# Adding the experts' biases in PSUM on VectorE instead of by small matmuls on TensorE, in a decoder layer with a mixture of experts

## What is computed

```python
def expert_block(args):
    xb, e = args
    gu = xb @ w_gu[e] + b_gu[e]
    x_glu = jnp.minimum(gu[:, 0::2], SWIGLU_LIMIT)
    x_lin = jnp.clip(gu[:, 1::2], -SWIGLU_LIMIT, SWIGLU_LIMIT)
    act = x_glu * jax.nn.sigmoid(SWIGLU_ALPHA * x_glu) * (x_lin + 1.0)
    return act @ w_dn[e] + b_dn[e]
```

## Time and profile before

| | |
|---|---|
| median of three runs | 2505.62 us (2504.82 to 2506.62) |
| the profiled execution, its own time | 2506.4 us |
| its span, first to last instruction | 2504.6 us |
| mean granted TensorE clock | 0.957 |
| TensorE busy | 2316.6 us, 92% |
| VectorE busy | 911.4 us, 36% |
| ScalarE busy | 349.1 us, 14% |
| GpSimd busy | 850.3 us, 34% |
| bytes moved by DMA | 521 MB, 208 GB/s over the span |
| first and last start of a matmul of the experts' first layer | 861.4 and 2466.6 us |

### The profile page before, as it was taken

The page is one execution under the profiler, slowest core; times in us unless marked ns, Lnnn a source line. Parts: engine busy times, 40 slices in busy tenths (PEclk is TensorE's granted clock), DMA queues, the critical chain, the costliest instruction groups (busy, mean ns, idle before and its releaser), DMA issues. The chain is left out here.

```text
span 2504.6 us, 84029 instructions
## 1 busy us (share of the span) xinstructions
PE 2316.6 (92%) x34310; PEld 1402.4 (56%) x34310; DVE 911.4 (36%) x3040; ACT 349.1 (14%) x927; POOL 850.3 (34%) x1649
## 2 busy tenths in 40 slices
PE   5899997999899299999999998999999999999994
PEld 3677885555544145464545565555555555555552
DVE  2212215776457423232323332333333333333333
ACT  0000004776511011000000000000000000000001
POOL 1000002554314523333333433334344343443433
PEclk8999997999999589999989999999999999999997
DMA  9421024000132472919393939395797799799994
GB/s 316 187 105 37 1 71 112 2 1 2 51 107 93 163 289 71 377 25 358 90 334 114 372 95 396 93 373 183 288 395 285 284 351 394 283 350 397 370 349 155
DMA packets 176316, 521.08 MB, mean 208 GB/s; under 512 B 26712, under 2 KB 56048, under 8 KB 176016
## 3 DMA queue, kind: packets, MB, share of 16 engines
q1 hardware_dynamic: 141504, 476.59, 49.7%
q0 software_dynamic: 33680, 40.20, 7.9%
q10 hardware_dynamic: 976, 2.23, 0.4%
HBM read 485.12 MB, written 32.30 MB: 207 GB/s over the span
## 5 line engine op out<-in xcount | busy, mean ns | idle before, releaser
L1540 PE MATMUL psum<-w_ring,xT 128*32 128x256 f32 x18304 | 1042.5, 382 | 7.4 <-DMA w_ring<-in_w_gate_up 7.4
L1540 PEld LDWEIGHTS psum<-w_ring,xT 128*32 128x32 f32 x18304 | 577.3, 111 | 402.4 <-DMA w_ring<-in_w_gate_up 14.4
L1552 PE MATMUL psum<-w_ring,actT 128*32 128x256 f32 x9152 | 537.4, 386 | 24.3 <-DMA w_ring<-in_w_down 24.0
L1552 PEld LDWEIGHTS psum<-w_ring,actT 128*32 128x32 f32 x9152 | 279.5, 111 | 243.2 <-DVE actT L1607 37.3
L1474 POOL TENSOR_TENSOR scalars<-scalars 128x1 f32<-128x1 f32 x578 | 110.4, 191 | 824.9 <-DVE xT L1611 624.9
L1598 DVE TENSOR_SCALAR glu<-psum 128x128 f32<-128x128 f32 x286 | 83.5, 292 | 618.1 <-PE psum L1540 607.2
L1590 ACT ACTIVATE sig<-glu 128x128 f32<-128x128 f32 x286 | 88.9, 311 | 1516.5 <-DVE glu L1598 1373.5
L1493 POOL DMA_INDIRECT x_rows<-y_out,scalars_i x145 | 233.9, 1613 | 40.6 <-issue 40.4
L1620 DVE SCALAR_TENSOR_TENSOR y_out<-psum,scalars,gate_q 128x256 f32<-128x256 f32 x143 | 69.2, 484 | 444.8 <-DMA x_rows<-y_out,scalars_i 224.1
L675 POOL TENSOR_SCALAR scores<-scores,coef 128x64 f32<-128x64 f32 (+5 forms) x128 | 132.8, 1053 | 160.6 <-DVE coef L887 160.6
L1483 POOL DMA_INDIRECT x_gathered<-h_rows,scalars_i x144 | 152.9, 1062 | 83.1 <-issue 83.1
(11 more groups left out here) (228 smaller groups left out, 1985.0 us busy)
## 6 DMA issues: line engine op xcount, KB each, us to landing
w_ring<-in_w_gate_up SPq DMA_DIRECT2D x256, 1024.0 KB
w_ring<-in_w_down SPq DMA_DIRECT2D x128, 1024.0 KB
ada<-in_w_ada SPq DMA_DIRECT2D x24, 1024.0 KB, 8.0
xt<-in_x SPq DMA_DIRECT2D x8, 512.0 KB, 7.0
w_uv_then_w_out<-in_w_in SPq DMA_DIRECT2D x4, 1024.0 KB, 12.8
x_rows_in<-in_x SPq DMA_DIRECT2D x8, 512.0 KB, 4.7
x_rows<-x SPq DMA_DIRECT2D x8, 512.0 KB, 2.9
h_rows<-h SPq DMA_DIRECT2D x8, 512.0 KB
```

Of the source, the lines that this page charges most:

```text
L1540: last = nc.tensor.matmul(psU[h][j * BLK:(j + 1) * BLK, :], xT[:, k, :], w[:, j], start=False, stop=(k == KD - 1))
L1552: last = nc.tensor.matmul(psO[m * BLK:(m + 1) * BLK, :], actT[h][:, k, :], w[:, m * Q:(m + 1) * Q], start=False, stop=(h == 1 and k == KD ...
```

## The change

The first half's bias and the second layer's are no longer made by matmuls. VectorE adds them to the PSUM tiles: `b_up` to `psU[0]` before `glu`, and `b_dn` to `psO` before `y_out`. Only the second half's bias stays on TensorE, so `bias` shrinks to [96, 1024], and `split_bias` works on a third of the columns. For VectorE each bias must stand in all 32 partitions of a strip. `load_bias` does that on ScalarE's queue: eight DMAs per expert, each repeating one row (or a part of it) over 32 partitions. There are two buffers of each. The first two experts' loads are issued before the loop; from the second expert on, each expert's program begins with the loads for the next one, behind a wait for the last `y_out` of the expert before, which was the last reader of that buffer. VectorE waits for an expert's loads before its blocks. Some semaphores of `route` are merged, to the same effect.

```diff
@@ route: SyncE's loads
         for i in range(3):
-            sp.dma_start(b_rows[i * E:(i + 1) * E, 0:2 * D], b_gate_up).then_inc(s_b, 16)
-            sp.dma_start(b_rows[i * E:(i + 1) * E, 2 * D:3 * D], b_down).then_inc(s_b, 16)
+            sp.dma_start(b_rows[i * E:(i + 1) * E, :], b_gate_up[:, D:2 * D]).then_inc(s_b, 16)
...
@@ experts
+    b_up, b_dn = two("up_bias", [P, Q]), two("down_bias", [P, Q])
...
@@ experts: tensor
         def up(e, h):
-            w_bias = bias[:, h * D:(h + 1) * D].rearrange("p (b j c) -> p j b c", b=4, j=4)
-            for j in range(4):
-                nc.tensor.matmul(psU[h][j * BLK:(j + 1) * BLK, :], select[:, e:e + 1].to_broadcast([3 * E, BLK]), w_bias[:, j], start=True, stop=False)
+            w_bias = bias[:].rearrange("p (b j c) -> p j b c", b=4, j=4)
+            if h:
+                for j in range(4):
+                    nc.tensor.matmul(psU[h][j * BLK:(j + 1) * BLK, :], select[:, e:e + 1].to_broadcast([3 * E, BLK]), w_bias[:, j], start=True, stop=False)
...
                 pe.wait_ge(s_y, n + AHEAD)
-                for m in range(4):
-                    at = 2 * D + m * Q
-                    nc.tensor.matmul(psO[m * BLK:(m + 1) * BLK, :], select[:, e:e + 1].to_broadcast([3 * E, BLK]), bias[:, at:at + Q], start=True,
-                                     stop=False)
                 for h in range(2):
                     pe.wait_ge(s_actT[h], n + 1)
                     down(e, h)
...
@@ experts: scalar
+        def load_bias(p, done=None):
+
+            at = bias_place(p)
+            which = act.value_load(order[0:1, p:p + 1], min_val=0, max_val=E - 1)
+            if done is not None:
+                act.wait_ge(s_y, done)
+            up = b_gate_up[bass.ds(which, 1), 0:D].rearrange("a (b j c) -> (a j) b c", b=4, j=4)
+            down = b_down[bass.ds(which, 1), :].rearrange("a (m c) -> (a m) c", m=4)
+            for q in range(4):
+                rows = slice(q * BLK, (q + 1) * BLK)
+                act.dma_start(b_up[at][rows, :].rearrange("p (b c) -> p b c", b=4),
+                              up[q].partition_broadcast(BLK)).then_inc(s_bias[at], 16)
+                act.dma_start(b_dn[at][rows, :], down[q].partition_broadcast(BLK)).then_inc(s_bias[at], 16)
...
+        load_bias(0)
+        load_bias(1)
         for e in range(E):
             b = first_of(act, e)
             many = many_of(act, e)
+            if 1 <= e < E - 1:
+                load_bias(e + 1, b + AHEAD)
             with act.Fori(0, many) as i:
...
@@ experts: vector
             dve.wait_ge(s_up[h], b + 1)
+            if h == 0:
+                nc.vector.tensor_tensor(psU[0], psU[0], b_up[at][:], ALU.add).then_inc(s_added, 1)
+                dve.wait_ge(s_added, 3 * b + 1)
             nc.vector.tensor_scalar(glu[:], even, LIMIT, None, ALU.min).then_inc(s_glu[h], 1)
...
             dve.wait_ge(s_dn, b + 1)
+            nc.vector.tensor_tensor(psO, psO, b_dn[at][:], ALU.add).then_inc(s_added, 1)
+            dve.wait_ge(s_added, 3 * b + 3)
             dve.wait_ge(s_ysc, 16 * b + 16 * AHEAD + 16)
             nc.vector.scalar_tensor_tensor(y_out[:], psO, w_cur[:], gate2[:], ALU.mult, ALU.mult).then_inc(s_y, 1)
...
             dve.wait_ge(s_ids, 2 * e + 2)
+            at = bias_place(e)
+            dve.wait_ge(s_bias[at], 128 * (e // 2 + 1))
             with dve.Fori(0, many) as i:
```

More of the change, by code:

```diff
@@ L96, in layer_kernel @@
         counts = keep("block_counts", [P, 3, E], i32)
-        bias = keep("bias_parts", [3 * E, 3 * D], bf16)
+        bias = keep("lin_bias_parts", [3 * E, D], bf16)
         select = keep("select", [3 * E, E], bf16)
@@ L129, in layer_kernel @@
         with ExitStack() as s4:
-            s_w = experts(nc, s4, sem, psum, w_gate_up, w_down, k_quarter, list_d, h2_d, x1_d, mod_d, counts, bias, select, order)
+            s_w = experts(nc, s4, sem, psum, w_gate_up, w_down, b_gate_up, b_down, k_quarter, list_d, h2_d, x1_d, mod_d, counts, bias, select, order)
         with ExitStack() as s5:
@@ L1154, in body @@
                 pe.wait_ge(s_mask, TILES - 3)
-                nc.tensor.matmul(psR[:, 0:E], ones[:], total_b[1][:], start=True, stop=True).then_inc(s_part, 1)
+                nc.tensor.matmul(psR[:, 0:E], ones[:], total_b[1][:], start=True, stop=True).then_inc(s_cnt, 1)
             project(t, 0)
@@ L1299, in _ @@
         dve.wait_ge(s_first, 5)
[L1300 to L1301 removed]
+        nc.vector.scalar_tensor_tensor(scale2[:], scale2[:], 1.0, g2[:], ALU.add, ALU.mult).then_inc(s_first, 1)
+        dve.wait_ge(s_first, 6)
         def place_experts():
             first, second = place_f[:, 0, :], place_f[:, 1, :]
[L1305 removed]
+            dve.wait_ge(s_cnt, 1)
             ch.link(nc.vector.scalar_tensor_tensor(key[:], psR[:, 0:E], float(E), iota_e,
@@ L1353, in _, with experts @@
         ch.link(nc.vector.tensor_copy(counts[:], blocks_f[:]))
-def experts(nc, ctx, sem, psum, w_gate_up, w_down, k_quarter, list_d, h2_d, x1_d, mod_d, counts, bias, select, order):
+def experts(nc, ctx, sem, psum, w_gate_up, w_down, b_gate_up, b_down, k_quarter, list_d, h2_d, x1_d, mod_d, counts, bias, select, order):
     sb = lambda name, shape, dt=f32: ctx.enter_context(nc.sbuf_tensor(name, shape, dt))
@@ L1391, in experts @@
     s_spent = [sem(f"w_spent{c}") for c in range(CHUNKS)]
+    s_bias = [sem(f"bias_rows_loaded{i}") for i in range(2)]
     s_rows, s_quarter, s_ids = sem("slot_rows_loaded"), sem("quarter_added"), sem("ids_ready")
@@ L1539, in up @@
                 for j in range(4):
-                    last = nc.tensor.matmul(psU[h][j * BLK:(j + 1) * BLK, :], xT[:, k, :], w[:, j], start=False,
+                    last = nc.tensor.matmul(psU[h][j * BLK:(j + 1) * BLK, :], xT[:, k, :], w[:, j], start=(h == 0 and k == 0),
                                             stop=(k == KD - 1))
@@ L1552, in down @@
                     last = nc.tensor.matmul(psO[m * BLK:(m + 1) * BLK, :], actT[h][:, k, :], w[:, m * Q:(m + 1) * Q],
-                                            start=False, stop=(h == 1 and k == KD // 2 - 1))
+                                            start=(h == 0 and k == 0), stop=(h == 1 and k == KD // 2 - 1))
                 if k % 2:
```

46 lines of the change are left out of this document (22 added, 24 removed).

## The result

The changed kernel takes 2554.12 us (median of four runs, 2549.72 to 2558.22), the kernel before 2506.12 beside it (2504.82 to 2509.12). The ratio is 1.0188, with a 95% interval of 1.0169 to 1.0208: slower by 48 us. The forecast was 2541, with 2493 to 2665 as its range. The profiled execution took 2549.7 us with a span of 2547.9; the one before had a span of 2504.6. So the two traces are 43.3 us apart, and the expert stage (from the first matmul on expert weights to the last) grew by 43.0, from 1608.5 to 1651.5 us. Everything happened there. The median of the four runs lies another 4.4 us above the profiled execution; no trace shows where, but the other three had mean granted clocks of 0.950 to 0.952, the profiled one 0.954.

The account below looks back on a forecast made before the run. The prediction took TensorE to bound the expert stage, through each block's own chain. Its terms, -14.5 - 2.6 + 46 + 6, came to +35 us on 2506.4, so 2541 us, with a range of 2493 to 2665.

Parts of the forecast that it names:

- First-half group: Expert blocks: removing the first half's bias matmuls saves TensorE 0.11 us in each of 132 blocks, 14.5 us gained.
- Second-layer group: Expert blocks: removing these bias matmuls gains only 0.02 us per block, 2.6 us, as TensorE then waits for the second actT.
- VectorE's additions: Before glu and y_out in each block: 0.51 us each, hidden behind other work, costing nothing.
- Issues in front of the sigmoid: Expert changes: ScalarE's eight issues, 4.56 us, delay the sigmoid; TensorE waits 2.1 us at 22 changes, 46 us lost.
- the 22 changes that the forecast counted: Of 30 expert changes with loads, those outside the waits for weights, each expected to stall TensorE 2.1 us.
- the shadow of the waits for weights: Eight changes, into experts 1 to 6, 9 and 10, where existing weight waits were taken to hide the stall.
- More traffic: Bias loads add 256 KB, 1.0 us, per expert, counting only where TensorE waits for weights: 6 us lost.
- the five known places: Five blocks whose second-layer rows show four weight waits each, the only places where added traffic was to cost.
- The clock: TensorE's clock falling behind stalls at expert changes: nothing in the sum; as a rival, 34 us more.
- the third rival: Each 2.1 us wait brings TensorE to half clock, 34 us more, 2576; chance with longer issues 0.17.
- The first rival: At expert changes ScalarE's issues also wait for SP's, taking 15.1 us in place of 4.56: 2772 us; chance 0.15.
- The second rival: ScalarE's issues fit their cover if y_out comes 2.1 us earlier against TensorE; kernel faster, 2495 us; chance 0.09.

Follow-up runs that it names:

- e6: Kernel before, with only the first layer's first-half biases moved to VectorE and four unheld loads per expert: 2505.2 us, ratio 0.9988.
- e7: Kernel before, with only the second layer's biases moved to VectorE and four loads per expert, waited for only ahead of their addition: 2510.7 us, ratio 1.0008.
- e4: Changed kernel without the bias loads from the third expert on, VectorE's additions kept: 2497.7 us, ratio 0.9972 to the kernel before.
- e8: Changed kernel without VectorE's two bias additions per block, loads and their place kept: 2553.0 us, ratio 1.0190 to the kernel before.
- e3: Changed kernel with each of the eight loads split into two of 16 rows, sixteen issues per expert change: 2667.6 us, ratio 1.0644 to the kernel before.
- e5: Changed kernel with loads issued behind the previous expert's last sigmoid, unheld: down_bias for the coming expert, up_bias for the one after: 2512.2 us, ratio 1.0016.
- e11: As e5, but from the third expert on each load writes 8 rows in place of 32: 2504.8 us, ratio 0.9980 to the kernel before.
- e1: Changed kernel with all eight loads of an expert issued behind the last sigmoid of the expert before it: 2688.0 us, ratio 1.0732 to the kernel before.
- e9: Kernel before, no loads: TensorE makes first-half bias rows once per expert, VectorE copies and adds them; other bias matmuls stay: 2496.0 us, ratio 0.9962.

## Why the prediction was right, and where it was not

- **First-half group, -14.5**: 0.11 us per block was right (0.113, e6). **Second-layer group, -2.6**: 0.02 was right (0.021, e7), and with it the reason, the wait for the second actT. The two came to 11.3 us without loads (e4), not 17.1: the 78 middle blocks gained 0.134 each, but the 28 last blocks only 0.07, the 23 first blocks away from the waits for weights nothing (0.2 us longer in all), and the blocks around those waits nothing steady.
- **VectorE's additions**: 0.43 us, not 0.51, and free (e8).
- **Issues in front of the sigmoid, +46**: right in its mechanism, and in the size of one stall; that the total came out is in part luck. Of the 22 changes that the forecast counted, 17 stalled, 35.6 us together, 2.1 each as reckoned, and five did not, since their y_out was early. In their place came five of the eight that were to lie in the shadow of the waits for weights: the one-block experts 1, 3, 5 and 9 stalled by 1.8 to 2.3 us each, 8.6 together, and expert 6 waited 1.1 us longer for actT. Behind the one-block experts, the first blocks of 2, 4, 6 and 10 did not take this in but grew by 0.2 to 1.5 us themselves, in part because rows asked for one block ahead landed late; only behind 4 and 6 the second block gave back 0.8 and 1.1. With longer stalls (e3) the waits do take some in: the four one-block experts are 7.2 to 8.6 us longer than before, and the two blocks behind each 3.0 to 5.4 us shorter. So even there the shadow covered half and not the whole. Why, no run tested alone. The time of the issues came out in the same way: they were 0.49 us apart when undisturbed, not 0.57, but 20 of the 240 took 0.8 to 1.5 us, so that from the end of y_out to the end of the last issue it was 4.56 us in the mean, the forecast's figure.
- **More traffic, +6**: too small where the loads stand well. e5 and e11 put it at some 11 us (9 of them from the rows), since it also costs in blocks outside the five known places.
- **The clock**: the third rival held in part. Four of 25 stalls brought a 3.4 us stretch of half clock, 1.2 to 1.7 us each, 6.3 us in all in their blocks; much of it came back in the next change, which had no stall. The forecast had none, and a whole 34 in the rival.
- **The first rival** (issues wait for SP's, 2772) fell: eight issues of 0.33 to 0.40 us beside SP's 8.07 us for three. The Trainium skill, Perfetto Trace Analysis, DMA Instruction — HWDGE, has a shared generator locked while in use; the trace agrees at most for the 20 long issues. All of these overlap an issue of SP, but so do 189 of the 220 others, which stayed under 0.75 us.
- **The second rival** (no cost of issuing, 2495) is about what e4 gave (2498, without the loads), so its sum was sound. Its condition, an early y_out, was met at five of the 30 changes, and there the issues did fit their cover. The Trainium skill, DMA: Bandwidth & Descriptors, Issuing engines are not separate DMA queues, calls the cost of issuing usually small; the trace differs: in e3, 240 more issues that move nothing more cost 113 us.

So the trace's 43.0 us stand against the forecast's 35 as follows: 12.4 us gained in middle and last blocks, not 17.1; 35.6 us of stalls away from the waits for weights, not 46; 6.3 for the clock, not in the sum; and 14.1 around the waits for weights, not 6 (0.6 us less is left over). The errors in part cancel. All this is read from one trace of each kernel, and I would not trust its parts to better than 2 or 3 us.

## What to carry to other kernels

An engine's queue is a place in time: the same eight issues cost 42 us less where nothing held them and nobody waited behind (e5), so ask of each what it waits for and who waits behind it. A load then has a second deadline, its landing, which beside large transfers was 8 to 10 us away for 32 KB (e1). The number of places that pay is a term by itself: here 22 were expected and 22 waited for actT, but five of them were others. And where rows repeat per group, making them once per group on the engine that has them (e9) can beat loading them.

## What was not expected

- The four 32 KB loads of down_bias in the last change of e1 land 2.5 us after their issue (median), with no weight transfers left; all 128 have a median of 10.1.
- A change of expert right behind one that lost 3.7 us or more had mostly no stall, as its y_out was early. Its cause is open.
- ScalarE's time for one issue grows with its rows, 0.33 us for 32 and 1.06 for 128; yet cutting to 16 does not shorten it (0.38), and with 8 it is 0.29.
- One 128-row DMA in place of four made the weights later (64 us of waits for 44). That it ran on four of the DMA engines is likely, and not tested.
- Single stalls of TensorE, 2.2 to 4.3 us long between stretches of full work, were followed by a stretch at 1.2 GHz in four of 25 cases.
